# A gated-MLP decoder layer on one core: w_down product with 17 of 44 k-pair steps in Strassen's scheme

## The reference

```python
h = rms_norm(x, ffn_norm_g)
u = causal_depthwise_conv(h @ w_up, conv_w, conv_b)
gate, val = jnp.split(u, 2, axis=-1)
x = x + (jax.nn.silu(gate) * val) @ w_down        # (256, 5632) @ (5632, 2048)
```

## Time and profile before

| | |
|---|---|
| time, median of 3 runs | 1466.62 us (1466.41 to 1467.03) |
| the profiled execution, its own time | 1466.32 us |
| its span | 1464.3 us |
| PE busy | 1455.5 us, 7688 matmuls |
| DVE busy | 932.5 us |
| ACT busy | 768.0 us |
| POOL busy | 431.1 us |
| granted TensorE clock, mean | 0.999 |

### The profile page before, as it was taken

How to read it: one execution, slowest core, us unless ns; L and a number is a source line. 1 busy time by engine, 2 the same in 40 slices (tenths; PEclk the granted TensorE clock), 3 DMA queues, 4 the chain that set the end, 5 groups by cost and what they waited for, 6 DMA issues and landing times.

```text
span 1464.3 us, 24546 instructions
## 1 busy us (share of the span) xinstructions
PE 1455.5 (99%) x7688; PEld 1246.4 (85%) x7688; DVE 932.5 (64%) x1205; ACT 768.0 (52%) x1063; POOL 431.1 (29%) x486
## 2 busy tenths in 40 slices
PE   8999999999999999999999999999999999999999
PEld 6888888888888888888888888888888888888887
DVE  6545455876655557765567778777777777545443
ACT  6544445576766766655454554454554555333332
POOL 1100000323222223550015555655555655000000
PEclk9999999999999999999999999999999999999999
DMA  7666665655555555575566666666666666655554
GB/s 243 194 181 186 186 180 165 193 179 177 158 167 158 158 169 176 186 246 186 186 186 177 198 188 186 185 187 194 193 188 192 179 191 198 201 194 191 190 197 147
DMA packets 130489, 272.09 MB, mean 186 GB/s; under 512 B 10784, under 2 KB 10816, under 8 KB 130192
## 3 DMA queue, kind: packets, MB, share of 16 engines
q1 hardware_dynamic: 129664, 269.12, 59.8%
q0 software_dynamic: 464, 2.42, 0.5%
q10 hardware_dynamic: 320, 0.01, 0.0%
HBM read 269.42 MB, written 2.10 MB: 185 GB/s over the span
## 4 chain that ended last, share of the span: by engine, by line
PE 99%; DVE 0%; DMA 0%; ACT 0%; issue 0%; POOL 0%; DVEq 0%; ACTq 0%; POOLq 0%
PE bank L1346 98%; PE bank L1395 0%; DMA rows_in<-in_attn_norm_g 0%; PE bank L1529 0%; DVE y L1103 0%; PE bank L1569 0%; DVE hT L765 0%; PE bank L1489 0%; ACT hi L417 0%; ACT hT L434 0%; POOL rows_in L1123 0%; DVE lo L740 0%; PE bank L1446 0%; PE bank L1419 0%; PE bank L1476 0%
## 5 line engine op out<-in xcount | busy, mean ns | idle before, releaser
L740 DVE TENSOR_TENSOR lo<-raw,hi 128x1024 fp32r<-128x1024 f32 (+1 forms) x508 | 651.0, 1285 | 425.0 <-ACT hi L417 424.2
L417 ACT ACTIVATE hi<-raw 128x1024 fp32r<-128x1024 f32 (+1 forms) x508 | 535.3, 1055 | 540.9 <-PE bank L1346 536.5
L1346 PE MATMUL bank<-h2T,hi 128*128 128x512 f32 x1408 | 482.8, 394 | 0.0
L1346 PE MATMUL bank<-h2T,lo 128*128 128x256 f32 x1408 | 376.4, 277 | 0.0
L1346 PEld LDWEIGHTS bank<-h2T,hi 128*128 128x128 f32 x1408 | 257.9, 188 | 53.4
L1346 PE MATMUL bank<-hT,hi 128*128 128x512 f32 (+1 forms) x784 | 274.4, 395 | 0.7 <-DVE lo L740 0.7
L1346 PEld LDWEIGHTS bank<-h2T,lo 128*128 128x128 f32 x1408 | 264.4, 188 | 7.8
L1346 PE MATMUL bank<-hi,ffT 128*128 128x512 f32 x704 | 216.8, 389 | 0.4 <-DVE y L1103 0.4
L1346 PE MATMUL bank<-hT,lo 128*128 128x256 f32 (+1 forms) x784 | 215.1, 284 | 0.0
L1346 PE MATMUL bank<-hi,hT 128*128 128x512 f32 x640 | 198.0, 390 | 0.0
L1310 POOL TENSOR_TENSOR u<-u,rms_row 128x256 f32<-128x256 f32 x88 | 121.3, 1378 | 237.9 <-DVE u L1041 220.6
(11 more groups left out here) (198 smaller groups left out, 1224.9 us busy)
## 6 DMA issues: line engine op xcount, KB each, us to landing
raw<-in_w_in SPq DMA_DIRECT2D x176, 512.0 KB, 3.6
raw<-in_w_up SPq DMA_DIRECT2D x176, 512.0 KB, 3.8
raw<-in_w_down SPq DMA_DIRECT2D x88, 512.0 KB, 3.4
raw<-in_w_branch SPq DMA_DIRECT2D x32, 512.0 KB, 3.7
raw<-in_w_out SPq DMA_DIRECT2D x32, 512.0 KB, 3.6
y<-in_x SPq DMA_DIRECT2D x4, 512.0 KB, 7.0
y<-in_x POOLq DMA_DIRECT2D x1, 2048.0 KB, 9.5
out<-y SPq DMA_DIRECT2D x8, 256.0 KB, 3.1
```

Of the source, the lines that this page charges most:

```text
L417: act.activation(hi[s][:, 0:width], raw[s][:, 0:width], ACT.Copy)\
L740: dve.tensor_tensor(lo[s][:, 0:width], raw[s][:, 0:width], hi[s][:, 0:width].bitcast(f32), ALU.subtract)\
L1346: return pe.matmul(o, l, r, start=start, stop=stop, skip_group_check=True)
```

## The change

The 44 tiles of k are taken in 22 pairs, and each half m runs over 22 steps of one pair. A plain step does what two chunks did before: 8 products. A summed step takes the 2 x 2 block product of the pair (2 token tiles and 2 k tiles on the left, 2 k tiles and 2 column groups on the right) in Strassen's scheme, in Winograd's form: 7 products, of sums of blocks. It takes four chunks' worth of hi/lo slots (the first of them half filled) instead of two: B1's left half; B2; `sum13` with two sums of weight blocks; `sum24` with two more. Half 0 has 7 summed steps and half 1 has 10, 17 of 44. The order is: steps 0 to 5 plain, then summed and plain in turn from 6 to 19, 20 to 22 plain, then summed and plain in turn from 23 to 42, 43 plain.

DVE makes the weight sums of a summed step (four 128x512 additions, `sums13` and `sums24`) during the plain step before it. SP may reuse a raw slot only when both the lo and the sums from it are done.

The sums on the left (`whole` = hi + lo, then four differences) are made once for each of the ten pairs, in six batches of one or two pairs, after steps 3, 7, 11, 15, 26 and 30 (`left_sums`), then ACT makes their hi parts (`left_hi_part`, after its hi copies of the same step), and one or two steps later DVE their lo parts (`left_lo_part`). One of them takes the place of the pair's own second token tile in ffT. They lie where h2T and the convolution's buffers were.

Four of the seven products go to one set of four banks (PARTIAL) and three to the set in which the plain steps accumulate (DIRECT); the sets A and B change roles between the halves. The partial products are added up by DVE after the half's last summed step: ACT copies the first, DVE adds 8 terms to y or to each other, and the four direct banks are added as before. That makes 12 additions per half instead of 4. ACT's, DVE's and SP's code for the stage is unrolled.

The diff at its core:

```diff
+    PAIRS = FT // 2
+    BATCHES = [(6, 2, 3), (8, 2, 7), (10, 2, 11), (12, 1, 15), (0, 2, 26), (2, 1, 30)]
+    SUMMED = [k + j for k, n, _ in BATCHES for j in range(n)]
+    Step = namedtuple("Step", "m pair made chunk raw")
+    def down_steps():
+        first = [(0, k, None) for k in range(6)]
+        rest = [k for k in range(13, PAIRS)]
+        for i in range(7):
+            first += [(0, SUMMED[i], i), (0, rest[i], None)]
+        first += [(0, k, None) for k in rest[7:]]
+        rest = [k for k in range(PAIRS) if k not in SUMMED]
+        second = [(1, rest[0], None)]
+        for i in range(10):
+            second += [(1, SUMMED[i], i), (1, rest[i + 1], None)]
+        second += [(1, rest[11], None)]
+        table, chunk = [], C_DOWN
+        for i, (m, pair, made) in enumerate(first + second):
+            table.append(Step(m, pair, made, chunk, C_DOWN + 2 * i))
+            chunk += 2 if made is None else 4
+        assert all(sorted(s.pair for s in table if s.m == m) == [*range(PAIRS)] for m in range(2))
+        return table, chunk
...
+    STEPS, C_END = down_steps()
+    S_LIST = [s for s in STEPS if s.made is not None]
+    S_COUNT = {s: i for i, s in enumerate(S_LIST)}
+    S_LAST = [[s for s in S_LIST if s.m == m][-1] for m in range(2)]
+    P_END = [STEPS[PAIRS].chunk, C_END]
+    ORDER = [["11p1", "12v5", "22v5", "u2", "u3", "11p2", "12v3", "21q4", "22e8", "12u2", "21u3",
+              "22u3"],
+             ["11p1", "12v5", "22v5", "u2", "u3", "12u2", "21u3", "22u3", "11p2", "12v3", "21q4",
+              "22e8"]]
+    def summed(m, name):
+        return len(ORDER[0]) * m + ORDER[m].index(name) + 1
...
+        sum13 = at("sum13", [2 * GRP], 104 * KB)
+        sum24 = at("sum24", [2 * GRP], 108 * KB)
+        left_at = [(112 + 3 * i if i < 7 else 186 + 3 * (i - 7)) * KB for i in range(len(SUMMED))]
+        FIRST_OF = [sum(n for _, n, _ in BATCHES[:b]) for b in range(len(BATCHES))]
+        leftb = [at(f"leftb{b}", [n, 3, 2, P], left_at[FIRST_OF[b]], f32r)
+                 for b, (_, n, _) in enumerate(BATCHES)]
+        whole = [at(f"whole{b}", [n, 2, S], left_at[FIRST_OF[b]])
+                 for b, (_, n, _) in enumerate(BATCHES)]
+        left_raw = [at(f"left_raw{b}", [n, 4, P], (108 if b == 0 else 196) * KB)
...
+            for i, step in enumerate(STEPS):
+                for k in range(2):
+                    if i < 2:
+                        wait_alone(sp, lo_done, step.raw + k - AHEAD)
+                    else:
+                        old = STEPS[i - 2]
+                        wait_alone(sp, lo_done, old.chunk + k + 1)
+                        if old.made is not None:
...
+                            wait_alone(sp, (sum13_done, sum4_done)[k], S_COUNT[old] + 1)
...
+            def down_hi(c, src, width=2 * GRP):
+                act.wait_ge(w_used, c - SLOTS + 1)
+                act.activation(hi[c % SLOTS][:, 0:width], src[:, 0:width], ACT.Copy)\
+                    .then_inc(hi_done, 1)
...
+            def left_hi_part(b):
+                k, n, _ = BATCHES[b]
+                act.wait_ge(left4_raw, b + 1)
+                if k < 6:
+                    act.wait_ge(w_used, STEPS[k + n - 1].chunk + 2)
+                act.activation(ff_pairs(k, n)[:, :, 0, 0, P:S], left_raw[b][:, :, 0, :], ACT.Copy)                    .then_inc(left_hi, 1)
+                act.activation(leftb[b][:, :, :, 0, :], left_raw[b][:, :, 1:4, :], ACT.Copy)                    .then_inc(left_hi, 1)
...
+            def down_summed(step):
+                down_hi(step.chunk, weights_in(step.raw), GRP)
+                down_hi(step.chunk + 1, weights_in(step.raw + 1))
+                act.wait_ge(sum13_done, S_COUNT[step] + 1)
+                down_hi(step.chunk + 2, sum13)
+                act.wait_ge(sum2_done, S_COUNT[step] + 1)
+                act.wait_ge(sum4_done, S_COUNT[step] + 1)
+                down_hi(step.chunk + 3, sum24)
...
+            for i, step in enumerate(STEPS):
+                if step.made is None:
+                    down_plain(step)
+                else:
+                    down_summed(step)
+                for b, (_, _, at_step) in enumerate(BATCHES):
+                    if i == at_step:
+                        left_hi_part(b)
+                if i in (19, 42):
+                    copy_p1(step.m)
...
+            def sums13(step):
+                for r in (step.raw, step.raw + 1):
+                    dve.wait_ge(w_landed[r % SLOTS], 16 * (r // SLOTS + 1))
+                if S_COUNT[step]:
+                    dve.wait_ge(lo_done, S_LIST[S_COUNT[step] - 1].chunk + 3)
+                b1, b2 = weights(step.raw), weights(step.raw + 1)
+                dve.tensor_tensor(sum13[:, 0:GRP], b1[:, 0:GRP], b1[:, GRP:2 * GRP], ALU.add)
+                dve.tensor_tensor(sum13[:, GRP:2 * GRP], b1[:, GRP:2 * GRP], b2[:, GRP:2 * GRP],
+                                  ALU.add).then_inc(sum13_done, 1)
+            def sums24(step):
+                n, b2 = S_COUNT[step] + 1, weights(step.raw + 1)
+                dve.wait_ge(sum13_done, n)
+                if n > 1:
+                    dve.wait_ge(lo_done, S_LIST[n - 2].chunk + 4)
+                else:
+                    dve.wait_ge(left_done, 2)
+                dve.tensor_tensor(sum24[:, 0:GRP], sum13[:, 0:GRP], b2[:, GRP:2 * GRP], ALU.add)\
+                    .then_inc(sum2_done, 1)
+                dve.wait_ge(sum2_done, n)
+                dve.tensor_tensor(sum24[:, GRP:2 * GRP], sum24[:, 0:GRP], b2[:, 0:GRP], ALU.add)\
+                    .then_inc(sum4_done, 1)
...
+            def left_sums(b):
+                k, n, _ = BATCHES[b]
+                f, d = whole[b], left_raw[b]
+                a = ff_pairs(k, n).bitcast(f32)
+                if b == 0:
+                    dve.wait_ge(w_used, C_DOWN)
+                if b == 1:
+                    dve.wait_ge(ffT_done, FT)
+                if b > 0:
+                    dve.wait_ge(left_done, 2 * b)
+                dve.tensor_tensor(f[:, :, :, :], a[:, :, :, 0, :], a[:, :, :, 1, :], ALU.add)                    .then_inc(whole_done, 1)
+                dve.wait_ge(whole_done, b + 1)
+                dve.tensor_tensor(d[:, :, 0, :], f[:, :, 0, P:S], f[:, :, 1, P:S], ALU.subtract)                    .then_inc(left1_raw, 1)
+                dve.tensor_tensor(d[:, :, 2, :], f[:, :, 0, 0:P], f[:, :, 0, P:S], ALU.subtract)                    .then_inc(left3_raw, 1)
+                dve.wait_ge(left1_raw, b + 1)
+                dve.tensor_tensor(d[:, :, 1, :], d[:, :, 0, :], f[:, :, 0, 0:P], ALU.subtract)                    .then_inc(left2_raw, 1)
+                dve.wait_ge(left2_raw, b + 1)
+                dve.tensor_tensor(d[:, :, 3, :], d[:, :, 1, :], f[:, :, 1, 0:P], ALU.add)                    .then_inc(left4_raw, 1)
+            def left_lo_part(b):
+                k, n, _ = BATCHES[b]
+                dve.wait_ge(left_hi, 2 * b + 2)
+                dve.tensor_tensor(ff_pairs(k, n)[:, :, 0, 1, P:S], left_raw[b][:, :, 0, :],
+                                  ff_pairs(k, n)[:, :, 0, 0, P:S].bitcast(f32), ALU.subtract)                    .then_inc(left_done, 1)
+                dve.tensor_tensor(leftb[b][:, :, :, 1, :], left_raw[b][:, :, 1:4, :],
+                                  leftb[b][:, :, :, 0, :].bitcast(f32), ALU.subtract)                    .then_inc(left_done, 1)
...
+            def down_plain(step, after):
+                for k in range(2):
+                    if step.chunk + k >= C_DOWN + AHEAD:
+                        down_lo(step.chunk + k, weights(step.raw + k))
+                    if after is not None:
+                        (sums13, sums24)[k](after)
...
+            def down_summed(step):
+                down_lo(step.chunk, weights(step.raw), GRP)
+                down_lo(step.chunk + 1, weights(step.raw + 1))
+                down_lo(step.chunk + 2, sum13)
+                down_lo(step.chunk + 3, sum24)
+            for i, step in enumerate(STEPS):
+                if step.made is None:
+                    after = STEPS[i + 1] if i + 1 < len(STEPS) else None
+                    down_plain(step, after if after is not None and after.made is not None
+                               else None)
+                else:
+                    down_summed(step)
+                for b, (_, _, at_step) in enumerate(BATCHES):
+                    if i == at_step:
+                        left_sums(b)
+                    if i == at_step + (1 if b == 0 else 2):
+                        left_lo_part(b)
+                if i == 20:
+                    add_p1(0)
+                    add_v5(0)
+                    make_u2_u3(0)
+                if i == PAIRS:
+                    add_direct(0)
+                if i == PAIRS + 2:
+                    add_u2_u3(0)
+            add_p1(1)
+            add_v5(1)
+            make_u2_u3(1)
+            add_u2_u3(1)
+            add_direct(1)
...
+            def down_summed(step):
```

(67 more changed lines are left out.)

107 lines of the change are left out of this document (83 added, 24 removed).

## The result

The changed kernel takes 1484.87 us (median of 4 runs, 1484.17 to 1485.80), against 1466.65 for the kernel before: 1.0124 times, 95% interval 1.0107 to 1.0142. That is +18.2 us; the prediction said +8.1 (1474.7) with a range to 1484.0.

What follows compares the result with a forecast made beforehand. The prediction took PE as the bound, busy 1455.5 of 1464.3 us. Fewer matmuls (-11.56), free banks at the changeover (-0.39) and waits behind the left sums (+20.0) gave +8.1: 1474.7 us for the median, range 1468 to 1484, own case 1470 to 1479.

Steps and rivals of the forecast that it cites:

- the detour: Left sums go DVE, ACT, DVE while PE lives on DVE's lead: 5.48 us for a batch of two pairs.
- the load term: Weight loads into slots freed by summed steps: land after 3.5 us, and landings up to 4.5 us cost nothing.
- DVE's slack between two batches: Per summed and plain step, DVE needs 8.8 us and PE 10.2 us, leaving DVE 1.4 us over.
- the first batch: Left sums after step 3, among plain steps: PE waits 2.1 us, bounds 0 and 4.1.
- The saving: 51 fewer matmuls on PE, 11.56 us less, and free banks at the halves' changeover, 0.39 us less.
- The detours of the other five: PE waits behind batches 2 to 6: 4.1, 4.3 and 4.3 us for two pairs, 2.6 each for one.
- (c): Rival: summed steps' loads land at 4.3 us or more, DVE falls behind in every pair: 1480 to 1486, chance 0.14.
- (a): The forecast itself, PE waiting behind the batches' detours: 1470 to 1479, chance 0.58.
- (b): Rival: PE's clock falls to half speed behind the waits, up to 9 us more: 1475 to 1483, chance 0.14.
- (d): Rival: DVE enters each batch with 5.5 us of lead and the detour is hidden: -11.95, 1454.7, chance 0.10.
- The tail, the additions to y, the changeover: Partial-product adds hidden; end after PE stays 2.73 us of additions plus stores; changeover gets free banks, -0.39 us.

Runs made afterwards that it cites:

- kernel without left sums and with late weight sums: Changed kernel without making the left sums (PE multiplies unsummed ffT parts) and with DVE's weight sums behind both lo parts of a plain step: 1454.47 us (0.9920).
- late weight sums: Changed kernel with DVE making both lo parts of a plain step first, then the four weight sums: 1478.46 us (1.0081).
- half loads: Changed kernel with each w_down load bringing 512 of its 1024 columns, the rest of the slot stale: 1475.65 us (1.0066).
- half loads, ACT later: Changed kernel with 512-column w_down loads and ACT's hi parts of batches 2 to 6 one step later: 1463.61 us (0.9981).
- the zero matmuls: Changed kernel with 14 or 6 matmuls of a zero operand in PE's queue before its wait behind five batches: 1486.88 us (1.0145).
- the last kernels: Among them: changed kernel with ACT's hi parts later, weight sums behind both lo parts, 15 summed steps and batches moved: 1462.97 us (0.9977).

## Why the prediction was wrong

The sign and the detour were right. What failed is the load term, and with it DVE's slack between two batches; the first batch was priced too low as well.

How late PE is can be counted. The kernel without left sums and with late weight sums keeps PE busy throughout; the n-th matmul of the stage there against the n-th matmul elsewhere, each from its stage's first, gives what PE lost, in us. A row runs to the next batch; the numbers are rounded. The columns are the profiled executions (1484.38, 1473.85 and 1463.73).

| batch, after step | forecast | changed kernel | half loads | half loads, ACT later |
|---|---|---|---|---|
| 1, step 3 | 2.1 | 3.7 | 3.7 | 3.7 |
| 2, step 7 | 4.1 | 6.6 | 3.9 | 2.5 |
| 3, step 11 | 4.3 | 6.1 | 3.5 | 1.3 |
| 4, step 15 | 2.6 | 3.3 | 1.8 | 0.1 |
| 5, step 26 | 4.3 | 6.6 | 4.9 | 1.3 |
| 6, step 30 | 2.6 | 3.6 | 1.9 | 0.1 |
| sum | 20.0 | 29.8 | 19.7 | 9.1 |

**The saving** (11.56 + 0.39): right; the kernel without left sums and with late weight sums measures 11.96.

**The first batch** (2.1): 3.7, inside the bounds that the text gave (0 to 4.1), and the same with short loads and with ACT's other parts moved. The text had up to 3.6 and took off what the slack would pay; by the 3.7 it paid nothing. This is 1.6 us of the miss.

**The detours of the other five** (17.9): right in order, number and length (5.28, forecast 5.48). With half loads they cost 16.0 us, of which some 1.5 is the fall of the clock behind the fifth. The text's own sum for loads of 3.0 us (+5.0) leaves 14.8 for them, so the mechanism holds where the loads are short. That the total with half loads (19.7) is so near the 20.0 forecast for loads of 3.5 is luck: a low first batch and shorter loads make up for each other. Of the 9.1 us that stay when ACT's parts are moved as well, 3.7 are the first batch, whose detour was left as it was, and 5.4 the others.

**The loads**: here it failed. "The second raw slot is free 1.1 us before PE enters it; 0.2 + 3.5 us later the next weights land, 1.0 us before DVE wants to sum them, so landings up to 4.5 us cost nothing." The next weights land 4.6 us after their issue: summed steps free two slots 1.1 us apart, the two loads overlap, and each takes longer. The margin of 1.0 is gone. With 4.6 the loop closes: in the changed kernel, 4.72 from the issue at 1257.83 to the sum at 1262.55, 3.68 to the end of the weight sums' slot at 1266.23, then (leaving the batch out) 0.60, 1.23 and 0.17 to the next issue, 10.4 us, against PE's 10.2. With 3.5 in place of 4.6 it would be 9.3, as an estimate. So the slack of 1.4 us per pair, from which DVE was to win its lead back between two batches, did not exist. The other five batches cost 26.1 us instead of 17.9: these 8.2 us and the 1.6 of the first are the miss of 9.8 (10.2 by the medians). In the 8.2 the loads and the slow clock behind three batches are not told apart by a run; filling the waits, which kept the clock up, gained nothing. The text named the sensitivity (+16.2 if every load took 4.3) and gave it to rival (c) as the ends of a range, while the sum went by the median of evenly spaced loads.

**Rivals.** (c), late landings, 1480 to 1486, gave the right time, on top of (a): DVE's weight sums wait in 16 of 17 pairs. But PE does not wait in every pair, as (c) had it: it lost 27.4 us in the two to four steps right behind each batch and 2.4 elsewhere. The late loads act by keeping DVE's lead from growing back before the next batch.

(b): the clock did fall (0.50 from 1272 to 1274), behind three waits of 3.4 us. In the changed kernel keeping it up gained nothing, since DVE was late at that point, as the text said against (b). Where the loads are short that does not hold: with half loads the step behind the fifth batch lost 2.4 us at 0.50, where those behind the second and third lost 0.9 at 1.00, and the runs with a lower mean clock are up to 3.2 us slower. With late weight sums they are too (1476.60 at 0.998, 1479.82 at 0.994). The Trainium skill ("TensorE: Matmul & The Clock Gate", section "HAM oscillation — how this bites in real kernels") says that waits between bursts of matmuls put the gate back to half clock each time. Here that is so behind the waits of 3.4 us (0.50) and not behind those of 1.95 and 1.22 (1.00); that the time would follow, which I took from it for rival (b), the changed kernel doesn't bear out.

(d), the detour hidden by plain running's lead, is what the last kernels approach by moving the batches.

**The tail, the additions to y, the changeover**: hidden as forecast. After PE's end come four additions in 2.73 us as before. DVE busy rose by 100.0 us; 110 was forecast.

Open: the 2.0 us more with the zero matmuls, and how the 8.2 us divide between the loads and the clock.

## What to carry to other kernels

A load time read from evenly spaced loads belongs to that spacing. When a change frees buffers in pairs, price the loads again, and close the loop "slot freed, load, work, slot freed" before counting on an engine's slack: if the loop is longer than the bound engine's period, there is no slack, and every disturbance stays. When work is added between two in-order engines, put each part behind what the other engine needs next; two such waits can hide each other, so test the edits together as well as alone. And count how far the bound engine has come, not only how long it was marked as idle.

## What was not expected of the hardware

Two 512 KB loads issued 1.1 us apart took 4.5 and 4.6 us, two issued 3.6 apart 3.2 and 3.5; halved to 256 KB the median was 2.6. GpSimd's additions on 256 columns beside DVE took 1.6 to 1.7 us, and two of DVE's 1024-column subtractions took 3.42 and, beside GpSimd's 1024-column addition, 4.55 in place of 2.35. In the changed kernel the granted clock fell to 0.50 behind PE's waits of 3.4 us and stayed at 1.00 behind one of 1.95; with half loads it fell behind a wait of 2.42 and not behind those of 2.63 and 2.41.
